# Interleaving sample and prompt attention units, and moving the diff-head norm onto token rows

## What is computed

```
p = attn_map(a1, k1) - lam * attn_map(a2, k2)
o_diff = einsum('bhqk,bkhd->bqhd', p, v)
o_diff = _rms(o_diff, dout_g) * (1.0 - lam_init)     # over the 128 channels of a head
o = concatenate([o_fox, o_diff]) @ w_out
h = h + o;  y = h + moe(_rms(h, g))                  # 32 experts, top 4, weights 1024x2048 and 1024x1024
```

## Time and profile before

| | |
|---|---|
| time, median of 3 | 1354.49 us (1353.02 to 1355.77) |
| profiled execution: its own time, its span | 1354.91 us, 1353.0 us |
| PE, DVE, ACT, POOL busy | 95%, 28%, 16%, 11% of the span |
| attention stage on PE | from about 176 to 356 us |
| first product of the MoE stage | 411 us |

### The profile page before, as it was taken

How to read it: one execution, slowest core, us unless ns; L and a number is a source line. 1 busy time by engine, 2 the same in 40 slices (tenths; PEclk the granted TensorE clock), 3 DMA queues, 4 the chain that set the end, 5 groups by cost and what they waited for, 6 DMA issues and landing times.

```text
span 1353.0 us, 16150 instructions
## 1 busy us (share of the span) xinstructions
PE 1288.7 (95%) x6083; PEld 573.3 (42%) x6084; DVE 377.3 (28%) x958; ACT 209.9 (16%) x524; POOL 145.0 (11%) x340
## 2 busy tenths in 40 slices
PE   6799999999998999999999999999999999999997
PEld 3344444565454433434344343443434344343432
DVE  3213223557252322213222121311212132121212
ACT  5111322346150101101001010100101010010100
POOL 0021300000004101011010110101011010101000
PEclk9899965579998999999999999999999999999998
DMA  8901440036525999999999999999999999999994
GB/s 286 323 29 74 174 168 1 0 128 226 209 70 210 431 427 427 428 429 429 428 430 428 428 429 429 428 428 430 428 428 430 428 429 428 430 428 427 429 426 183
DMA packets 54537, 447.06 MB, mean 330 GB/s; under 512 B 10817, under 2 KB 11090, under 8 KB 29922
## 3 DMA queue, kind: packets, MB, share of 16 engines
q1 hardware_dynamic: 54498, 446.54, 79.4%
HBM read 441.66 MB, written 4.86 MB: 330 GB/s over the span
## 4 chain that ended last, share of the span: by engine, by line
PE 65%; DMA 25%; SPq 4%; DVE 2%; POOL 1%; issue 1%; ACT 1%; DVEq 0%; POOLq 0%; ACTq 0%
DMA arena<-in_w_gate_up 23%; PE psum L1588 17%; PE psum L1556 16%; PE psum L1537 7%; PE psum L1303 5%; PE psum L1451 3%; PE psum L1407 3%; PE psum L1603 2%; PE psum L1359 2%; SPq L390 2%; PE psum L1387 1%; PE psum L1339 1%; PE psum L1571 1%; PE psum L1567 1%; PE psum L1355 1%; SPq L406 1%
## 5 line engine op out<-in xcount | busy, mean ns | idle before, releaser
L1556 PE MATMUL psum<-arena 128*64 128x512 f32 x2048 | 450.5, 599 | 18.9 <-DMA arena<-in_w_gate_up 18.4
L1556 PEld LDWEIGHTS psum<-arena 128*64 128x64 f32 x2048 | 152.9, 138 | 314.7 <-issue 314.7
L1588 PE MATMUL psum<-arena 128*64 128x512 f32 x1024 | 224.8, 597 | 0.8
L1210 DVE TENSOR_SCALAR arena<-psum 128x256 f32<-128x256 f32 x64 | 26.7, 418 | 432.4 <-PE psum L1556 430.6
L1588 PEld LDWEIGHTS psum<-arena 128*64 128x64 f32 x1024 | 78.8, 138 | 136.0 <-issue 134.6
L1303 PE MATMUL psum<-arena 128*128 128x512 f32 x288 | 127.6, 599 | 0.0
L838 ACT ACTIVATE arena<-arena 128x256 f32<-128x256 f32 x64 | 26.7, 418 | 630.5 <-DVE arena L1210 630.5
L1537 PEld LDWEIGHTS psum<-arena 128*128 128x128 f32 x768 | 88.5, 194 | 16.1 <-issue 16.1
L1537 PE MATMUL psum<-arena 128*128 128x128 f32 x768 | 91.6, 279 | 3.8 <-POOL arena L604 3.8
L1603 PE MATMUL psum<-arena 128*128 128x512 f32 x192 | 93.2, 623 | 0.0
L597 POOL COPY arena<-arena 128x6 f32 (+1 forms) x16 | 3.0, 188 | 775.6 <-PE psum L1588 703.5
(11 more groups left out here) (215 smaller groups left out, 905.2 us busy)
## 6 DMA issues: line engine op xcount, KB each, us to landing
arena<-in_w_gate_up SPq DMA_DIRECT2D x128, 2048.0 KB, 25.0
arena<-in_w_down SPq DMA_DIRECT2D x64, 2048.0 KB, 22.6
arena<-in_w_in SPq DMA_DIRECT2D x6, 2048.0 KB, 19.6
arena<-in_cache_fox_k SPq DMA_DIRECT2D x8, 512.0 KB, 3.5
arena<-in_cache_diff_k SPq DMA_DIRECT2D x8, 512.0 KB, 4.4
arena<-in_cache_fox_v SPq DMA_DIRECT2D x8, 512.0 KB, 4.0
arena<-in_cache_diff_v SPq DMA_DIRECT2D x8, 512.0 KB, 5.6
arena<-in_w_out SPq DMA_DIRECT2D x4, 1024.0 KB, 7.5
```

Source lines behind the costliest of these rows:

```text
L1556: last = mm(banks[n][half], XT[u][:, k, half], piece_slot(s[x])[:, c0:c0 + 512], start=False, stop=(k == 7), skip_group_check=True)
L1588: last = mm(banks[hf][half], actT[:, 4 * i + c, half], w, start=False, stop=(i == 1 and c == 3), skip_group_check=True)
```

## The change

`att` is built anew: diff prompt units come first, then fox prompt units, and after each two of them stands one sample unit. Diff prompt outputs are now computed with tokens on partitions (probabilities are the stationary operand), like sample outputs. For both, ScalarE squares a 128x128 tile and accumulates over channels in one instruction, GpSimd computes mean plus epsilon and a power of -0.5 on 128x1, VectorE multiplies rows while it copies them out (`rows_evac`), PE transposes them (`turn_out`, now also for 8 prompt units), and VectorE multiplies by the gain (`o_evac`). `turn_out(i-3)` moves to the head of the pass. The all-ones products and the wide roots and reciprocals are gone.

```diff
+        for n, two in enumerate([(diff_p + fox_p)[i:i + 2] for i in range(0, 32, 2)]):
+            att += two + [sample[n]]
...
-            sp.wait_ge(d_done, DIFF_H)
...
+            def inverse_root(i):
+                n = rms_no[i]
+                ms, r = stat[:, 2 + n % 2:3 + n % 2], stat[:, 4 + n % 2:5 + n % 2]
+                g_.wait_ge(o_sq, n + 1)
+                nc.gpsimd.tensor_scalar(ms, stat[:, n % 2:n % 2 + 1], 1.0 / (2 * HD), EPS, ALU.mult, ALU.add
+                                        ).then_inc(o_ms, 1)
+                g_.wait_ge(o_ms, n + 1)
...
+                nc.gpsimd.tensor_tensor(r, ms, stat[:, 44:45], ALU.pow).then_inc(o_rt, 1)
...
+            def square_rows(i):
...
+                nc.scalar.activation(osq, banks[6 + turn_no[i] % 2][:, 0:P], ACT.Square,
+                                     accum_out=stat[:, n % 2:n % 2 + 1]).then_inc(o_sq, 1)
...
+            def rows_evac(i):
...
+                if rows_no[i] >= 1:
+                    ve.wait_ge(o_turned, rows_no[i])
+                if x["g"] == 1:
+                    n = rms_no[i]
+                    ve.wait_ge(o_rt, n + 1)
+                    nc.vector.tensor_scalar(o_rows, O[:, 0:P], stat[:, 4 + n % 2:5 + n % 2], None, ALU.mult
+                                            ).then_inc(o_copied, 1)
...
-                    nc.vector.tensor_scalar(dsq[:, h], banks[4][:, 0:SEQ], 1.0 / (2 * HD), EPS, ALU.mult, ALU.add
-                                            ).then_inc(d_ms, 1)
...
-                    link(nc.vector.reciprocal(dsq[:, h - 1], dsq[:, h - 1]))
...
-            for i in range(-3, NA + 2):
+            for i in range(-3, NA + 3):
+                if i - 3 in rows_no:
+                    turn_out(i - 3)
...
-                if 0 <= i - 2 < NA and att[i - 2]["where"] == "s":
-                    turn_out(i - 2)
...
-                    mm(banks[4][:, 0:SEQ], C["ones"], dsq[:, h], start=True, stop=True).then_inc(d_sum, 1)
...
-            mm(banks[3], C["ones"], dsq_s, start=True, stop=True).then_inc(d_sum, 1)
```

More of the change, by code:

```diff
@@ L117, in build @@
         consts_all = at(base, cur - base)
-        bs = C["causal"]
+        bs = at(base + sum(n for k, n in CONSTS[:[k for k, _ in CONSTS].index("cumul")]), 128)
         def take(n):
@@ L305, in stores_on @@
             return sum(1 for i in o_before(u, parity) if is_st(units[i]))
-        att = []
[L309 to L318, removed]
+        fox_p = [dict(where="p", g=0, h=h, qt=qt, nk=META + P * (qt + 1), turn=True)
+                 for h in range(FOX_H) for qt in range(2)]
+        diff_p = [dict(where="p", g=1, h=h, qt=qt, m=m, nk=META + P * (qt + 1), turn=m == 1)
+                  for h in range(DIFF_H) for qt in range(2) for m in range(2)]
+        sample = [dict(where="s", g=g, b=b, nk=NKEY_S, turn=True, s=2 * b + g) for b in range(BATCH_D) for g in range(2)]
+        att = []
+        for n, two in enumerate([(diff_p + fox_p)[i:i + 2] for i in range(0, 32, 2)]):
+            att += two + [sample[n]]
         NA = len(att)
@@ L323, in build, with by_rows @@
         NT = len(turns)
+        def by_rows(x):
+            return x["turn"] and (x["where"] == "s" or x["g"] == 1)
+        rows_no = {i: n for n, i in enumerate(i for i, x in enumerate(att) if by_rows(x))}
+        rms_no = {i: n for n, i in enumerate(i for i, x in enumerate(att) if by_rows(x) and x["g"] == 1)}
+        copies = [turn_no[j] for i in range(NA + 3) for j in (i - 3, i - 1)
+                  if 0 <= j < NA and att[j]["turn"] and by_rows(att[j]) == (j == i - 3)]
+        copy_no = {e: n + 1 for n, e in enumerate(copies)}
         def turns_upto(i):
@@ L567, in _, with keys @@
             g_.wait_ge(s_store[1], 16 * stores_on(NU, 1))
-            for s in range(2 * BATCH_D):
+            nc.gpsimd.memset(stat[:, 44:45], -0.5)
+            def keys(s):
                 b, g = s // 2, s % 2
@@ L763, in _ @@
                     turn_evac(i)
[L765 to L778, removed]
+                if i - 1 in rms_no:
+                    square_rows(i - 1)
             def square(t):
@@ L1406, in mix @@
                         v = V[:, place, g, vc] if place < 2 else v3[0][0:META, g, vc]
-                        last = mm(dst, v, pt[0:n, place], start=(n_ == 0), stop=(n_ == len(tiles) - 1))
+                        first, final = n_ == 0, n_ == len(tiles) - 1
+                        if g == 0:
+                            last = mm(O[64 * (h % 2):64 * (h % 2) + 64, 0:P], v, pt[0:n, place], start=first, stop=final)
+                        else:
+                            last = mm(O[:, 0:P], pt[0:n, place], v, start=first, stop=final)
                 else:
```

97 lines of the change are left out of this document (41 added, 56 removed).

## The result

The changed kernel takes 1420.68 us (median of 4 runs, 1405.37 to 1423.58), the kernel before 1353.99 us beside it: a ratio of 1.0468 (of the means; the medians give 1.0493), 95% interval 1.0435 to 1.0501. By the medians it is slower by 66.7 us. The prediction said 1410 us and slower. The profiled execution took 1423.58 us, the longest of the four, with a span of 1421.8 us.

The account below looks back on a forecast made before the run. Attention stage bound by PE at half clock: 184.5 + 206.8 work + 9.6 waits + 3 pipeline = 403.9 us, 54.7 later; +1.7 at `project_out`, -0.9 ones product: +55.5 on 1354.91, so 1410 us, range 1392 to 1424.

Parts of the forecast that it names:

- the step on which all hung: Attention stage: mixed prompt and sample units leave PE at granted clock 0.50 (1.2 GHz) throughout; chance 0.55.
- 1.7 us of loss: Start of `project_out`: it stays at half clock for some 3 us, losing about 1.7 us.
- The first rival: Attention stage: the mixture gets full clock, stage ends at 325 us, 24 earlier; whole time 1330 us; chance 0.20.
- the waits for VectorE: PE behind `turn_out` in the attention stage: 8 x 1.2, about 9.6 us, between 0 and 16.
- The second rival: Attention stage: clock comes up for a part and falls again; 1370 us, 1345 to 1392; chance 0.17.
- The sum: Attention stage at half clock: PE work 206.8 us plus waits and pipeline, ending at 403.9 us.
- filling and emptying: Attention stage's pipeline: 3 us added to the stage's end.
- eight key transposes: Sample units on PE at half clock: 1.90 us per set.
- the wait at the start: Attention stage's start: first sample key transposes wait for the `out_diff_v_s` store, so work counts from 184.5 us.
- the three terms that I had taken between bounds: PE at half clock: mixes 1.5 us (0.92 to 1.84), diff sample probability transposes 1.4 (0.8 to 1.6), `turn_out` 0.25 (at most 0.34).
- the third rival: Row norm: a GpSimd power of 4 us or more delays 16 units by 1 us or more; 1425 us or more; chance 0.05.
- The saving beside the samples: Four sample units lose table loads and a reciprocal: at most four times 3 us, already counted in the stage's work.

Follow-up runs that it names:

- e4_rows128: e1_v_first with prompt scores read from 128 partitions instead of 64, which alters the attention values; attention stage ends at 325.0 us, whole time 1675.65 us not usable.
- e8 to e10: Three runs on the kernel before: all prompt products on 128 rows plus five start products, 1320.82 us; those five alone, 1359.44 us; the rows alone, 1328.00 us.
- e1_v_first: Changed kernel with SP's V loads moved ahead of the wait for key transposes and the K load; 1404.47 us.
- e7_filler: Kernel before with unread 128-row products added, four in the attention stage's first pass and one in each of 29 passes after; 1372.58 us.
- e10_all_padded: Kernel before with all prompt products, scores and gates, on 128 rows by zero padding, no added products; 1328.00 us.
- e11_filled: e8_padded_burst plus one unread 128x256 product in each of the 15 passes beside the diff prompts; 1315.35 us.
- e5_q_padded: Kernel before with q zero-padded to 128 rows for the prompt scores, except the first two units; 1347.08 us.
- e2_old_order: Changed kernel's norm on token rows, with attention units in the order of the kernel before; 1359.33 us.
- e8_padded_burst: Kernel before with all prompt products zero-padded to 128 rows and five unread 128x512 products at the attention stage's start; 1320.82 us.
- e12_filled_norm: e11_filled with the norm on token rows, in the old order of units; 1315.14 us.

## Why the prediction was right, and what was off

**The clock, the step on which all hung: right.** I took 0.50 for the whole stage, and every stretch of the profiled execution shows it, until `project_out` had run for 3.2 us (the clock rose at 421.7 us; 1.7 us of loss were in the sum, 1.6 came). The reason that I gave, prompt scores on 64 and 8 rows beside the key transposes, was only argued there; e4_rows128 shows it for the scores, with the same instructions on more rows, and e8 to e10 show it from the other side. What I did not see is that the mixture leaves 0.50 in some executions: e1_v_first reached 0.66 in one stretch, and one of the four executions of the changed kernel, 1405.37 us, spent some 48 us less at 0.50 by its mean clock (0.916). So the step holds for most of the stage and not for all of it. The rule of the Trainium skill, TensorE: Matmul & The Clock Gate, "Why this matters for your kernels", that an engine kept busy without gaps keeps its full clock, is contradicted by this case: 0.50 at 90.00 us busy in 90 (e7_filler). In this stage wide products made the difference (e4_rows128, e10_all_padded), though not everywhere alone: the diff prompts of the old order needed fillers as well (e11_filled).

**The first rival** gave 325 us for the stage end if the mixture had the full clock. e4_rows128, which comes near that clock, ends at 325.0 us, with the V loads already moved. So its condition failed and its price came out to the microsecond, in part by luck: of the stage in e4_rows128, by the clocks shown, some 22 us were still at half clock, which the rival did not have, while the waits for VectorE came to 17.8 us where it had 23.

**The second rival** was to be ruled out by the Trainium skill, TensorE: Matmul & The Clock Gate, "Part 4: PE-mode transpose", which says that transposes do not count for the clock. The runs speak further against it: the clock of e5_q_padded came up at 274 us, right behind two sets of eight key transposes with one unit's scores between. No run had transposes alone, so it is not settled. In parts the rival came true, in e1_v_first (0.60 and 0.66 for 40 us).

**The sum.** Without the V waits the stage would end at 418.5 - 16.7 = 401.8 us, against 403.9 predicted. PE's own work from 184.4 us on was 210.2 us, where the sum had 206.8 and 3 for filling and emptying. By terms, all at half clock and from start to start: eight key transposes 1.84 us (1.90 predicted); the 24 mixes 1.59 (1.5); the six probability transposes of a diff sample unit 1.72 (1.4, and at most 1.6); `turn_out` 0.27 before key transposes and 0.41 before scores (0.25, and at most 0.34); the waits for VectorE 6.9 us in 12 (9.6 in 16); the wait at the start 5.6 us, to 184.4 us, as predicted. Two of the three terms that I had taken between bounds lie above their upper bound, and the waits and the filling below what I took. The sum is nearer than its terms because these errors have opposite signs.

**The step that failed is one that the sum did not have:** the prediction followed PE, VectorE and GpSimd into the new order but not SP's queue, though SP's loop ties the K load of one sample and the V load of another into one line of waits. That cost 16.7 us in four waits. e1_v_first removes all four by moving four lines; 14.7 us of them are won, since waits for VectorE take back 2. With the 16.7 us the forecast would have been 1427 us, 6 above the measured median and 3 above the profiled execution; without it the 1410 was 11 below. That the range held all the same owes something to its width: the V loads were in none of its terms.

**The norm on rows.** GpSimd's power took 0.55 us and PE never waited for it, so the third rival is out. The saving beside the samples, "at most four times 3 us", is real but small (2.0 us of the stage in e2_old_order, mostly at full clock), and the waits at `turn_out` in the diff half, 5.4 us there, take back more than that.

## What to carry to other kernels

When the order of work changes, walk every queue through the new order, the one that only issues DMAs too: two loads that had passes to spare can come to stand behind one another's condition. Read the granted clock beside the busy share: TensorE at 100% busy and 0.50 was freed here by making its narrow products wider, with zeros. With a few products added at the start and beside the diff prompts, that was worth 3% here, where reordering the same narrow work cost 5%. Widen all the narrow kinds of a stretch before judging (the scores alone gave 0.5%, scores and gates 2%), and then read the clock by stretch again: here it still fell where VectorE bounds the diff prompts, until filler products stood there too.

## What the runs showed of the hardware that was not expected

- PE busy for 90.00 us in 90 at a granted clock of 0.50 (e7_filler, 210 to 300 us), busy for 15.58 us in 20 at 0.90 (e4_rows128) and for 7.40 us in 10 at 1.00 (e12_filled_norm).
- Rows that hold zeros count: with scores and gate products on 128 rows the clock rose from 0.50 at about 209 us in pure fox prompts (e10_all_padded), with the same values computed.
- Fillers of 128 rows between products of 64 and 8 rows did not hold the clock past about 203 us, and the run took 18 us more than the kernel before (e7_filler). Fillers between products of 128 rows did (e11_filled).
- The clock fell about 0.5 us after a wait of 1.36 us (e8_padded_burst, e10_all_padded) and did not fall after one of 1.51 us (e12_filled_norm, with fillers).
- Scores on 128 rows with PE busy for 18.0 us in 20 did not raise it (e5_q_padded, 250 to 270 us).
